# Eight-core hybrid attention layer: casting loads for two constants, an early role read, and new rules and prices in the planner that orders the kernel

## The reference

```python
h = rms_norm(x, g_in)
(c_q, c_kv, k_pe, z_mla, q_swa, k_swa, v_swa, z_swa, q_mem, z_mem) = split_cols(h @ w_in, IN_SIZES)
y_mla = mla_attention(c_q, c_kv, k_pe, ...) * silu(z_mla)   # 8 heads, low-rank q/kv, rotary key, chunk-causal
y_swa = swa_attention(q_swa, k_swa, v_swa, sinks, rel_table) * silu(z_swa)  # banded, 8 heads
y_mem = memory_attention(q_mem, rms_norm(mem, g_mem), w_mem_kv) * silu(z_mem)  # 256 memory tokens
y = concatenate([y_mla, y_swa, y_mem]) @ w_out
return rms_norm(x + y, norm_final)
```

## Time and profile before

| | us |
|---|---|
| median of 3 runs | 866.05 (864.5 to 866.47) |
| the profiled execution, its own time | 863.48 |
| its span, slowest core (0) | 861.9 |
| spans of cores 0 to 7 | 861.9, 822.3, 789.2, 840.7, 861.9, 823.9, 789.8, 837.5 |
| core 0 busy: TensorE, VectorE, ScalarE, GpSimd | 686.8 (80%), 383.9 (45%), 344.7 (40%), 199.3 (23%) |

### The profile page before, as it was taken

One profiled execution on the slowest core, in us unless ns is written; L12 is line 12 of the kernel. 1 busy time (PEld: TensorE's weight loads), 2 busy tenths in 40 slices (PEclk: granted clock), 3 DMA queues, 4 the chain that ended last, 5 costly groups with the idle time before them and its releaser, 6 DMA issues.

```text
span 861.9 us, 10986 instructions; the slowest of 8 cores (789.2 to 861.9 us)
## 1 busy us (share of the span) xinstructions
PE 686.8 (80%) x3452; PEld 319.6 (37%) x3514; DVE 383.9 (45%) x524; ACT 344.7 (40%) x535; POOL 199.3 (23%) x184
## 2 busy tenths in 40 slices
PE   0436768999899699888889888878557799999991
PEld 0112335555344133444444334333223244444440
DVE  0461422262352654223444458586276754434331
ACT  1253301110460567444454466666436632222220
POOL 2087711010000002211521116464165520000000
PEclk9977879999999689999999999999869999999996
DMA  9999891061003133711100000000919653332121
GB/s 214 248 228 229 192 172 21 1 134 39 2 5 69 25 52 67 195 25 25 34 1 1 0 17 19 13 22 14 184 33 278 162 173 135 146 135 83 64 85 70
DMA packets 17764, 77.83 MB, mean 90 GB/s; under 512 B 2700, under 2 KB 3600, under 8 KB 14104
## 3 DMA queue, kind: packets, MB, share of 16 engines
q0 software_dynamic: 6768, 32.25, 21.2%
q1 hardware_dynamic: 10920, 44.69, 15.2%
HBM read 94.21 MB, written 11.53 MB: 123 GB/s over the span
## 4 chain that ended last, share of the span: by engine, by line
PE 48%; DVE 12%; DMA 12%; ACT 11%; issue 7%; POOL 4%; another core or an unknown queue 2%; SPq 2%; DVEq 0%; ACTq 0%; POOLq 0%
PE psd L646 48%; ACT ze_r L615 6%; DMA xms_r<-xm 6%; DMA qv_r<-qu_r 3%; DVE acc_r L618 3%; DVE z_r L618 3%; DMA kw_r<-ku_r 3%; POOL p_r L618 1%; POOL gA_r L618 1%; ACT pmb_r L615 1%; ACT sq_r L615 1%; DVE gA_r L618 1%; ACT rim_r L615 1%; SPq L1745 1%
## 5 line engine op out<-in xcount | busy, mean ns | idle before, releaser
L646 PE MATMUL psd<-x_r,w_r 128*128 128x512 bf16 (+1 forms) x1315 | 273.9, 364 | 20.7 <-DVE z_r L618 17.2
L646 PEld LDWEIGHTS psd<-x_r,w_r 128*128 128x128 bf16 x1344 | 129.7, 98 | 161.8 <-issue 36.9
L615 ACT ACTIVATE pmb_r<-psd 128x768 bf16<-128x768 f32 (+2 forms) x80 | 67.2, 874 | 47.2 <-DVE acc_r L618 19.2
L646 PE MATMUL psd<-x_r,wkv_r 128*128 128x512 bf16 (+1 forms) x190 | 45.0, 399 | 51.2 <-DVE x_r L637 33.4
L646 PE MATMUL psd<-wo_r,gA_r 128*128 128x512 bf16 x346 | 82.5, 379 | 0.7 <-DVE xo_r L618 0.3
L615 ACT ACTIVATE junk_r<-xo_r 128x512 f32<-128x512 f32 x44 | 27.7, 629 | 106.1 <-DVE xo_r L618 100.9
L615 ACT ACTIVATE ze_r<-z_r 128x512 f32<-128x512 f32 (+1 forms) x48 | 28.4, 593 | 101.4 <-DVE z_r L618 76.9
L618 DVE TENSOR_TENSOR xo_r<-psd,xo_r 128x512 f32<-128x512 f32 x44 | 30.3, 690 | 67.6 <-PE psd L646 66.1
L615 ACT ACTIVATE ze_r<-ze_r 128x512 f32<-128x512 f32 (+1 forms) x96 | 56.8, 593 | 7.6
L195 POOL DMA_DIRECT2D w_r<-wti x28 | 15.8, 568 | 172.7 <-PE psd L646 79.3
L646 PE MATMUL psd<-pmb_r,V_r 128*128 128x384 bf16 (+3 forms) x182 | 36.9, 327 | 19.8 <-POOL pmb_r L1351 15.7
(11 more groups left out here) (143 smaller groups left out, 901.8 us busy)
## 6 DMA issues: line engine op xcount, KB each, us to landing
w_r<-wti POOLq DMA_DIRECT2D x28, 512.0 KB, 9.1
xo_r<-xo SPq DMA_DIRECT2D x11, 1024.0 KB, 6.1
out<-xo_r SPq DMA_DIRECT2D x22, 512.0 KB, 2.6
xs_r<-xu SPq DMA_DIRECT2D x8, 1024.0 KB, 19.5
wo_r<-wo POOLq DMA_DIRECT2D x4, 2048.0 KB, 19.6
w_r<-wmk POOLq DMA_DIRECT2D x8, 512.0 KB, 23.5
xs_r<-xu SPq DMA_DIRECT2D x4, 768.0 KB, 58.2
wkv_r<-wkv POOLq DMA_DIRECT2D x4, 512.0 KB, 21.8
```

What stands on the lines that cost most here:

```text
L615: self.P.op("act", lambda e: e.activation(out=out, in_=in_, func=func, **kw), reads, writes, 0.19 + n / 1200.0)
L646: ins = e.matmul(out, lhsT=l, rhs=r, start=s0, stop=s1, skip_group_check=True)
```

## The change

`id` and `sel` are loaded by the POOL queue straight into their bf16 tiles; the f32 tiles and two VectorE casts go. Each engine reads its role before the shared first instructions. The corner memset is VectorE's alone. In the planner: an operation that several engines may run is taken on one only if none of the others would end it more than 0.01 us earlier; cross-engine latencies go from 0.1 to 0.2 us up to 0.2 to 0.3; a bank counts as free 0.6 us later; GpSimd's price of a gain goes from 1.4 to 3.2 cycles an element; TensorE's columns from 2400 to 2350 a us; DMAs cost 3.3 us a MB, the small ones too, behind their queue, and a DMA that is not a load ends 1.0 us after its queue rather than 2.0.

```diff
-    LAT = {"pe": 0.2, "act": 0.12, "dve": 0.1, "pool": 0.15}
+    LAT = {"pe": 0.3, "act": 0.2, "dve": 0.2, "pool": 0.25}
...
-                        t = max(bfree[b], bfree[b + 1])
+                        t = max(bfree[b], bfree[b + 1]) + 0.6
...
-                        t = (bfree[b], not held[b ^ 1])
+                        t = (bfree[b] + 0.6, not held[b ^ 1])
...
                     s = max(free[e], o.est[e])
+                    fin = s + o.eng[e][1]
+                    if len(o.eng) > 1 and any(max(free[x], o.est[x]) + o.eng[x][1] < fin - 0.01 for x in o.eng):
+                        continue
...
-                if o.mb < 0.1:
-                    o.end = fin + 2.2
-                else:
-                    t = max(fin + 1.2, qfree[e])
-                    both = max(0.0, max(qfree["pool" if e == "sp" else "sp"], 34.0) - t)
-                    d = o.mb * 3.1
-                    qfree[e] = t + (2 * d if 2 * d <= both else d + both / 2)
-                    o.end = qfree[e] + 2.0
+                t = max(fin + 1.2, qfree[e])
+                both = max(0.0, max(qfree["pool" if e == "sp" else "sp"], 34.0) - t)
+                d = o.mb * 3.3
+                qfree[e] = t + (2 * d if 2 * d <= both else d + both / 2)
+                o.end = qfree[e] + (2.0 if o.load else 1.0)
...
-        self.P.op({"dve": (fn, (n / 2 + 151) / 960.0), "pool": (fn, n * 1.4 / 960 + 0.1),
+        self.P.op({"dve": (fn, (n / 2 + 151) / 960.0), "pool": (fn, n * 3.2 / 960 + 0.1),
...
-        c = sum(max(x[5], 60) / 2400.0 + 0.0025 for x in lst)
+        c = sum(max(x[5], 60) / 2350.0 + 0.0025 for x in lst)
...
-                P.op({"pool": (fn, 0.2), "dve": (fn, 0.25)}, None, [], [pbp], rows=(64, 128))
+                P.op("dve", fn, [], [pbp], 0.22)
...
-        idt, idp = P.new("id", [128, 128], F32)
-        P.dma("sp", idt[:, :], self.dr["idn"][:, :], writes=[idp], mb=.06, what="id")
         ib, self.idbp = P.new("idb", [128, 128], BF16)
         self.idb = ib[:, :]
+        P.dma("pool", ib[:, :], self.dr["idn"][:, :], writes=[self.idbp], mb=.06, what="id")
...
-        self.cp(ib[:, :], idt[:, :], [idp], [self.idbp], 128)
...
-        sf, sfp = P.new("self", [4, 128], F32)
-        P.dma("sp", sf[:, :], self.dr["sel"][:, :], writes=[sfp], mb=.01, what="sel")
         sl, self.selp = P.new("sel", [4, 128], BF16)
         self.sel = sl
-        self.cp(sl[:, :], sf[:, :], [sfp], [self.selp], 128)
+        P.dma("pool", sl[:, :], self.dr["sel"][:, :], writes=[self.selp], mb=.01, what="sel")
...
-        progs[0].replay(eng, e, 0, n)
         e.reg_load(hi, role_d[0:1, 0:1])
         e.reg_load(lo, role_d[0:1, 1:2])
+        progs[0].replay(eng, e, 0, n)
```

## The result

The changed kernel takes **831.04 us** (829.37 to 833.68) against 866.05: 35 us less, ratio 0.960 [0.956, 0.965]. The forecast was 852 with a range of 838 to 874; the sign was right, the size was not.

The account below looks back on a forecast made before the run. Core 0 sets the time: DMA transfers bound it until about 97 us, then waits and latency in the sweep. Terms 6-2-4-4-7-4+1 = -14 gave 849.5 us profiled, 852 median; range 838 to 874.

Parts of the forecast that it names:

- Role read first: At the start, four role reads now precede the first loads and delay them: +6 us, bounds 3.5 to 10.
- Identity and sel cast by the load: At the start, VectorE's wait goes and the head's matmuls end earlier, but under the DMA bound: 0 us.
- Gains: After the third unit's x lands, gains move from GpSimd to VectorE and ScalarE: -2 us (0 to -4).
- The stall before the rotary key: VectorE's 8.9 us stand before a swap's product, with TensorE behind it, halves: -4 us (0 to -8).
- Banks and latencies in the projections: In the projections, a quarter of TensorE's 17.4 us of z waits goes: -4 us (0 to -17).
- GpSimd's share of the sweep: In the sweep, GpSimd's p, oc and gA partly move to faster VectorE, some queueing: -7 us (0 to -14).
- Less sharing: In the sweep, VectorE's acc sums quicken as GpSimd does less beside them: -4 us (0 to -9).
- Memsets on VectorE: 24 memsets move from GpSimd to VectorE, a quarter of their time on the chain: +1 us (0 to +5).
- The swap stall: In the sweep, swaps and wo loads meet again, so the 14.5 us wait stays: 0 us (0 to -18).
- Rival B: The new order also parts swaps from wo loads, 18 us less, cut off by core 3: 840 us, chance 0.20.
- The floor by core 3: Core 3 ends at 845 us by the median's scale; its own gains bring perhaps 5, limiting the total to 840.
- Rivals C and D: C: one new in-order stall, +15, 875 us, chance 0.24. D: role read costs 10, half the gains queue, 866, 0.14.

Follow-up runs that it names:

- no_role: The changed kernel with the role read after the shared first loads, as before the change: 827.15 us.
- best_role_late: wo_after_swaps with the role read after the shared first loads, as before the change: 801.72 us.
- only_start: The kernel before with only the casting loads of id and sel and the early role read: 868.43 us, ratio 1.005.
- no_bank: The changed kernel without the bank slack (banks free after 0.1 us, as before): 847.85 us.
- only_bank: The kernel before with only the bank slack added (banks free 0.6 us later): 857.51 us.
- wo_dep: The changed kernel with the wo loads waiting for the last pair's rotary queries: 843.10 us.
- no_pool: The changed kernel with no tensor-tensor work on GpSimd: 818.57 us.
- wo_after_swaps: The changed kernel with no tensor-tensor work on GpSimd, swap DMAs not chained, and wo loads behind the last rotary queries: 806.13 us, again 803.73.

## Why the prediction was wrong

Against the sum of -14 stand -35 us. By its own steps:

- *Role read first, +6.* Right in kind, and high: the four reads took 3.1 us, near the low bound of 3.5, and no_role shows 3.9, best_role_late 2.0. That the third unit's last x would come at 101 to 107 us was wrong (95.0).
- *Identity and sel cast by the load, 0.* Too small ahead of the third unit: the stretch to its last x is 5.5 us shorter, and only_start and no_role point to this edit. The term looked at VectorE's wait and not at what is loaded ahead of x. What it is worth at the end is open: together with the role read it costs 4 us (only_start).
- *Gains, -2.* The first matmul of the third unit comes 3.3 us after the landing, 3.8 before: 0.5 us.
- *The stall before the rotary key, -4.* 4.6 us by the trace, from the unit's first matmul to the own projections, but not as said: VectorE's stall went only from 8.9 to 8.15. TensorE's wait is 2.6 us shorter, and about as much comes from the rotary key's matmuls, which now run before the clock falls. The number was luck in part.
- *Banks and latencies in the projections, -4.* The z waits fell by 7.0 us (forecast: a quarter of 17.4, 4.4), but the stage is only 0.6 us shorter, because others grew (TensorE's for pw from 2.7 to 6.1 us, for cqf from 2.2 to 5.3). So the forecast for the start, 6 - 2 - 4 - 4 = -4, met -7.9, which is 3.3 - 5.5 - 0.5 - 4.6 - 0.6; its largest term was not in the sum.
- ***GpSimd's share of the sweep*, -7, and *Less sharing*, -4: the step that failed.** It had the two at half of their ends, 14 and 9, since VectorE, busy 131 of 190 us, would make moved work queue. The rule, which holds this step and little else, takes 15 to 20 us of the sweep on core 0 with the long wait and the output blocks left out, and 21 us of the kernel alone. A third of the acc sums' time as excess was right (16.6 of 46.2 us). What was wrong is the halving and its reason: VectorE was busy so long in part because it shared, and work moved to it made room for itself; with all of it moved VectorE is busy less, 123 us of a sweep against 129. On the chain the acc sums fell by 15 us, from 25.6 to 10.9. The two terms themselves are not parted by a run.
- **The bank slack: priced in one place only.** The term weighed it against the z waits in the projections. But the score banks pass between TensorE and ScalarE in the same way, 13.3 us of TensorE's waits on core 0 and 30.3 on core 1, which the sum had at nothing without a reason. On core 0 the slack takes 5 to 6 us of the sweep by the table above, and 4.5 us behind it by no_bank. In all it is 17 us by no_bank and 8 by only_bank. Latencies, which shared this term, are worth nothing measurable.
- *The stage behind the sweep, "nothing to take there".* It is 5.1 us shorter, of which 3.7 are output blocks that now run inside the sweep.
- *Memsets on VectorE, +1.* Not told apart from the rest by a run; the 44 memsets take 0.165 us each, where the 24 on GpSimd took 0.23. TensorE's wait behind a memset is still there, by VectorE now (18.5 us), as said.
- *The swap stall, 0.* Right, place and cause: it meets the wo loads again, 11.9 us. Rival B (that the order parts them) didn't happen, though the time went below B's 840.
- *The floor by core 3, 845 us.* Wrong. It took 5 us as core 3's own gain, and it was 71. Cores 1 to 3 have the same GpSimd work and the same bank waits in longer sweeps; core 1's sweep went from 325.8 to 286.7 us. So the cut-off that kept B, and the low end of the range, at 838 to 840 was not there.
- Rivals C and D, a new stall or no change, didn't come. wo_dep shows that C's mechanism exists in this planner: one edit, a new hole of 20.6 us, 12 us slower than changed.

What stays open: each edit makes one new order of the whole program, and a few us of each figure may be that order's luck (the slack is 8 or 17, the rule 21 or 15, by what else is in place). The sweep's last column takes two pieces of that luck out; with one order for each edit the rest can't be parted from the mechanisms, above all in the columns ahead of and behind the sweep. Not tried either: the loads of identity and sel by themselves, and how early wo must be issued, without meeting the swaps, for its last 6 to 8 us of waiting to go.

## What to carry to other kernels

An engine whose work makes a faster neighbour's instructions longer should be costed by that too: read the quickest instance of an instruction against its mean, shape by shape, and take that difference times its count as an estimate of the room that moving the work makes. Before comparing a stage across runs, take out what each order places anew, here one long wait and the next stage's blocks: the slack's part of the sweep shows only then. Price a planner's slack at every place where the resource passes between two engines, not just where the largest named wait is, and look at the other cores for the same pattern before calling them a floor. A hole beside a weight load moves with the load: look for the next user of that load before delaying it.

## What the runs showed of the hardware

- Two-input sums on VectorE without and with GpSimd's two-input work beside them (no_pool, before): 256 columns f32 0.42 and 1.01 us, 1024 columns 1.23 and 1.75 us.
- A swap of 64 KB from SBUF to SBUF lands in 2.0 us (median, wo_after_swaps) when no big load is under way; with two 2 MiB casting loads issued 1.2 us earlier on the other queue it takes 8.7 us, and swaps issued together are used 21 us after. The Trainium skill, page DMA: Bandwidth & Descriptors, section Anatomy of one DMA, has a fixed cost of about 2.0 us for a DMA issued by GpSimd. The swaps are issued by SyncE, and their first number is the same; the second is not setup but the loads ahead, since wo_after_swaps, with the loads behind the swaps, has VectorE waiting 0.17 us for the product.
- A register load from DRAM takes 0.47 to 1.1 us with idle queues, against up to 5.7 us under the first loads. The 0.47 lies under the floor of about 0.6 us that the prediction names.
- The same 16 matmuls of 384 columns take 2.79 us at the full granted clock, 2.4 GHz (changed), and 5.30 us behind a wait of 8.19 us, nearly all at 1.2 GHz (before, mean 0.53).
